# Expert blocks that gather and scatter token rows, and a final norm by token tiles

## The reference

```python
def hierarchical_moe(h, w_rg, b_rg, w_re, b_re, w_gate, w_up, w_down):
    p_g = softmax(hf @ w_rg + b_rg)                  # 4 groups
    g_sel = argmax(p_g); p_gsel = p_g[g_sel]
    e_logits = (hf @ w_re + b_re)[group g_sel]       # 8 experts of the group
    top_p, top_i = top_k(softmax(e_logits), 2)
    weights = top_p / sum(top_p) * p_gsel
    ...                                              # rows sorted by expert
    hid = silu(xb @ w_gate[e]) * (xb @ w_up[e])      # 1024 -> 512
    y = hid @ w_down[e]                              # 512 -> 1024
    out[token] += y * weight

x = x + g_f * hierarchical_moe(h, ...)               # g_f: 1024 gates
return rms_norm_2(x, final_norm_g)                   # x * rsqrt(mean(x*x) + eps) * g
```

## Time and profile before

| | us |
|---|---|
| median of 3 runs | 2663.51 (2662.41 to 2669.47) |
| the profiled execution, its own time | 2671.42 |
| its span in the profile | 2669.7 |
| TensorE busy | 2448.4 (92%) |
| VectorE busy | 814.4 (31%) |
| ScalarE busy | 472.3 (18%) |
| GpSimd busy | 35.3 (1%) |
| mean granted clock of TensorE | 0.955 of full speed |

### The profile page before, as it was taken

The page is one execution under the profiler, slowest core; times in us unless marked ns, Lnnn a source line. Parts: engine busy times, 40 slices in busy tenths (PEclk is TensorE's granted clock), DMA queues, the critical chain, the costliest instruction groups (busy, mean ns, idle before and its releaser), DMA issues. The chain is left out here.

```text
span 2669.7 us, 22222 instructions
## 1 busy us (share of the span) xinstructions
PE 2448.4 (92%) x8196; PEld 1209.4 (45%) x8196; DVE 814.4 (31%) x1821; ACT 472.3 (18%) x1005; POOL 35.3 (1%) x50
## 2 busy tenths in 40 slices
PE   6999899999999999989999999999994798888883
PEld 4444544444444655554444444645554333333331
DVE  4444331212123265552121221377423000000004
ACT  2322111110002154431111000112311010000000
POOL 0000000000000000000000000000001000000001
PEclk9999799999999899989999999999996899999996
DMA  8434113433342111214843343321006679999992
GB/s 329 173 142 163 74 63 126 163 151 127 131 184 103 56 56 55 81 64 159 328 176 138 126 164 151 126 91 36 1 0 262 257 323 428 428 429 428 428 401 111
DMA packets 50482, 482.53 MB, mean 181 GB/s; under 512 B 4928, under 2 KB 4928, under 8 KB 25296
## 3 DMA queue, kind: packets, MB, share of 16 engines
q1 hardware_dynamic: 36784, 430.85, 40.6%
q0 software_dynamic: 10112, 38.80, 3.8%
q10 hardware_dynamic: 3488, 11.58, 1.1%
HBM read 444.47 MB, written 36.74 MB: 180 GB/s over the span
## 5 line engine op out<-in xcount | busy, mean ns | idle before, releaser
L1021 PE MATMUL ps<-big,ring 128*128 128x512 f32 x1024 | 448.9, 596 | 3.6 <-PEq L932 1.5
L963 PE MATMUL ps<-hT,ring 128*128 128x512 f32 x1024 | 444.2, 594 | 0.0
L1021 PEld LDWEIGHTS ps<-big,ring 128*128 128x128 f32 x1024 | 192.6, 191 | 245.6 <-issue 245.6
L963 PEld LDWEIGHTS ps<-hT,ring 128*128 128x128 f32 x1024 | 193.9, 191 | 237.8 <-issue 236.6
L2529 PE MATMUL ps<-ring,big 128*64 128x512 f32 (+1 forms) x768 | 259.4, 603 | 25.1 <-ACT big L2575 10.8
L576 PE MATMUL ps<-hT,ring 128*128 128x512 f32 x384 | 174.8, 606 | 2.1 <-ACT hT L428 2.1
L2529 PEld LDWEIGHTS ps<-ring,big 128*64 128x64 f32 (+1 forms) x768 | 92.2, 154 | 156.6 <-issue 136.5
L2529 PE MATMUL ps<-big 128*64 128x512 f32 (+1 forms) x384 | 143.2, 625 | 19.1 <-DMA oT<-in_up 7.5
L1715 PE MATMUL ps<-hT,ring 128*128 128x512 f32 x320 | 142.4, 600 | 2.7 <-DVE big L2097 1.7
L206 DVE SCALAR_TENSOR_TENSOR tmp<-ring,cact,tmp 128x512 f32<-128x512 f32 (+1 forms) x192 | 131.6, 685 | 6.8
L2611 DVE TENSOR_TENSOR big<-big,ps 128x512 f32<-128x512 f32 x20 | 13.7, 687 | 349.4 <-ACT big L2579 333.0
(11 more groups left out here) (414 smaller groups left out, 2474.0 us busy)
## 6 DMA issues: line engine op xcount, KB each, us to landing
ring<-in_stream SPq DMA_DIRECT2D x99, 2048.0 KB, 8.8
ring<-in_gate SPq DMA_DIRECT2D x18, 2048.0 KB, 27.5
ring<-in_up SPq DMA_DIRECT2D x17, 2048.0 KB, 28.0
ring<-in_down SPq DMA_DIRECT2D x13, 2048.0 KB, 29.9
big<-in_down SPq DMA_DIRECT2D x10, 2048.0 KB, 29.4
big<-in_up SPq DMA_DIRECT2D x8, 2048.0 KB, 28.4
slot_rows<-zero POOLq DMA_DIRECT2D x2, 7424.0 KB, 38.6
big<-in_gate SPq DMA_DIRECT2D x6, 2048.0 KB, 30.4
```

Source lines behind the costliest of these rows:

```text
L963: last = pe.matmul(m.ps[:, j, :], w[:, k, j * P:(j + 1) * P], m.hT[:, k, :], start=(k == 0), stop=(k == KT - 1))
L1021: last = pe.matmul(m.ps[:, bank(half, j), :], w[:, k, j * P:(j + 1) * P], hid[:, 8 * c + k, :], start=(c == 0 and k == 0), stop=(c == 3 an ...
```

## The change

- Row tables. `m.d_xt` holds the 512 token rows in order, stored by ScalarE (`m.written`); there is no table of slots. The routing builds a table of places on TensorE: for each of 29 blocks and each of its 128 rows the token, the row of `m.d_yt` (token, or token + 512 for the second choice) and the weight. A place with no row gets 4096, which is beyond the bound, and its row isn't moved.
- Each block gathers its rows from `m.d_xt` by an indirect DMA on GpSimd, scales its output by weight and gate on VectorE and scatters it to `m.d_yt` by an indirect DMA on GpSimd. Only `m.d_yt` is filled with zeros, 4 MB.
- Block 0's rows are picked on TensorE by a matmul with a 0/1 matrix, and its gate and up products run inside the routing phase. The last block isn't scattered: TensorE spreads it by a 0/1 matrix to the four token tiles.
- Four weight loads go out in the residual phase (`HELD_EARLY`). The logits run with the feature tile in the outer loop. The group's Exp stands before the row evictions on ScalarE. Ranks come from comparisons with the expert on partitions, no longer from cubes.
- During blocks 1 to 8 TensorE turns the residual tile by tile to token rows. The rows of `m.d_yt` are loaded by SP and added before the last block's.
- The final norm goes by token tiles: ScalarE squares and sums a tile, VectorE scales it, SP stores it (0.5 MB). The output is now stored as tokens x features. The order of the last two blocks is `down(18)`, `front(19)`, `down(19)`, and the loads follow it.
- The overflow phase is rewritten with nine unrolled blocks and one set of buffers; it still doesn't run on this data.

```diff
@@ phase_residual
             def _(sp):
                 prefetch(m, sp, name)
+                if name == "out_m":
+                    for i in range(HELD_EARLY):
+                        load_expert(m, sp, i)
@@ phase_route, TensorE
-                keep_busy(m, pe, 5, 7)
-                for i in range(NT):
-                    for k in range(KT):
-                        pe.wait_ge(h_ok, k + 1)
+                for k in range(KT):
+                    gated = pe.matmul(..., m.mod2[:, 40 + k:41 + k].to_broadcast([P, P]), ident, ...)
+                for k in range(KT):
+                    pe.wait_ge(h_ok, k + 1)
+                    for i in range(NT):
...
+                pe.matmul(m.ps[:, 0, 0:NT * EXPERTS], con(m, "tri_strict"), whole, start=True, stop=True)
+                pe.matmul(m.ps[:, 1, 0:NT * EXPERTS], m.ones[:], whole, start=True, stop=True).then_inc(counted, 1)
...
+                pe.wait_ge(picked, NT)
+                for k in range(KT):
+                    for i in range(NT):
+                        last = pe.matmul(m.ps[:, 4 + k // 4, ...], rows[:, i, k * P:(k + 1) * P], pick[:, i, :], ...)
+                for j in range(2):
+                    pe.wait_ge(m.wfull[j], 16)
+                    for k in range(KT):
+                        if j == 0 and k == 2:
+                            for n in range(2 * NT):
+                                pe.wait_ge(tables, 1 + n // NT)
+                                last = pe.matmul(m.ps[:, 7, 0:3 * PL], row_of[:, n, :], table[:, n, :, :], ...)
+                            last.then_inc(tabled, 1)
+                        pe.matmul(m.ps[:, 2 + j, :], xt0[:, k * P:(k + 1) * P], bufs[j][:, k * 512:(k + 1) * 512], ...)
@@ phase_route, ScalarE
+                act.wait_ge(eg, 1)
+                act.activation(ge, ge, ACT.Exp).then_inc(expd, 1)
                 for i in range(NT):
                     act.activation(rows[:, i, :], ..., ACT.Copy).then_inc(ev, 1)
+                    act.dma_start(m.d_xt[i * P:(i + 1) * P, :], rows[:, i, :]).then_inc(m.written, 16)
-                act.wait_ge(eg, 1)
-                act.activation(ge, ge, ACT.Exp).then_inc(expd, 1)
@@ phase_route, GpSimd
-                        pool.indirect_dma_start(m.d_xs, bass.IndirectOffsetOnAxis(ap=m.idx[:, c:c + 1], axis=0),
-                                                rows[:, i, :], None).then_inc(m.scattered, 16)
+                pool.wait_ge(m.written, 16 * NT)
+                pool.wait_ge(xpick, 2)
+                pool.wait_ge(slotted, 1)
+                for t in (1, 2):
+                    gather_rows(m, pool, gathered_rows(m)[:, t % 2, :], PLACES[t]).then_inc(m.xin[t % 2], 16)
@@ phase_experts, GpSimd
-                    pool.dma_start(xb[:, t % 2, :], block_rows(m.d_xs, t)).then_inc(xin[t % 2], 16)
+                    if 3 <= t + 2 < BLOCKS:
+                        pool.wait_ge(xtr, t + 1)
+                        gather_rows(m, pool, xb[:, t % 2, :], PLACES[t + 2]).then_inc(m.xin[t % 2], 16)
+                    if t < last:
+                        pool.wait_ge(ya, t + 1)
+                        pool.wait_ge(yb, t + 1)
+                        pool.indirect_dma_start(m.d_yt, ..., y[:, t % 2, :], None, bounds_check=2 * T - 1,
+                                                oob_is_err=False).then_inc(yo[t % 2], 16)
@@ phase_experts, SP, behind the weight loads
+                sp.wait_ge(dn, last)
+                for i in range(NT):
+                    for j in range(2):
+                        sp.dma_start(yrows[j][:, i, :], m.d_yt[j * T + i * P:...]).then_inc(yin[i], 16)
+                tail.store(sp, 0)
@@ phase_experts, TensorE
+                    if 1 <= t <= KT:
+                        for i in range(NT):
+                            ins = pe.transpose(m.ps[:, 1, ...], m.xT[:, t - 1, i * P:(i + 1) * P], ident)
...
-                front(0)
                 for t in range(BLOCKS):
-                    if t + 1 < BLOCKS:
+                    if 1 <= t + 1 < last:
                         front(t + 1)
+                    elif t == last:
+                        front(t)
                     down(t)
+                for h, done in enumerate((ya, yb)):
+                    pe.wait_ge(done, BLOCKS)
+                    for i in range(NT):
+                        pe.matmul(m.ps[:, 2 * i + h, :], spread[:, i * P:(i + 1) * P], y[:, ..., h * 512:(h + 1) * 512], ...)
@@ phase_experts, VectorE
+                    for h, done in enumerate((ya, yb)):
+                        dve.scalar_tensor_tensor(y[:, s, ...], m.ps[:, 6 + h, :], m.wt[:, PLACES[t]:...],
+                                                 gate_rows(m)[:, ...], ALU.mult, ALU.mult).then_inc(done, 1)
...
+                for i in range(NT):
+                    dve.wait_ge(yin[i], 32)
+                    for j in range(2):
+                        c1.link(dve.tensor_tensor(token_rows(m, i), token_rows(m, i), yrows[j][:, i, :], ALU.add))
+                rows_out(last)
+                for h in range(2):
+                    for i in range(NT):
+                        dve.wait_ge(loose, NT * h + i + 1)
+                        add_rows(m, dve, i, h).then_inc(joined, 1)
+                        if h and i:
+                            tail.scaled(dve, i - 1, 0)
+                tail.scaled(dve, NT - 1, 0)
+class FinalNorm:
+    def squares(self, act, joined, before):
+        for i in range(NT):
+            act.activation(..., token_rows(m, i), ACT.Square, accum_out=m.st[:, i:i + 1]).then_inc(self.squared, 1)
+            act.activation(m.st[:, i:i + 1], m.st[:, i:i + 1], ACT.Sqrt, bias=m.eps[:, 0:1], scale=1.0 / D)
+    def scaled(self, dve, i, again):
+        dve.reciprocal(m.st[:, i:i + 1], m.st[:, i:i + 1]).then_inc(self.inverse, 1)
+        dve.scalar_tensor_tensor(self.out[:, i, :], token_rows(m, i), m.st[:, i:i + 1], final_gain(m), ALU.mult, ALU.mult)
@@ build
             lambda: phase_overflow(nc, m),
-            lambda: phase_combine(nc, m),
-            lambda: phase_norm(nc, m, "h", [(fl(m, "final_norm2"), None, None, m.hT)]),
-            lambda: phase_store(nc, m, out),
+            lambda: phase_stored(nc, m),
```

More of the change, by code:

```diff
@@ L2235, in _ @@
                 dve.reciprocal(m.st[:, 0:16], m.st[:, 0:16])
+HELD_EARLY = 4
 def load_order():
@@ L2300, in phase_route @@
     sc = take(NT * 8).rearrange("p (j i) -> p j i", j=8)
-    cnt, over, start, tmp32, incl, key, rank, base, cap, jump = (take(EXPERTS) for _ in range(10))
+    cnt, over, start, tmp32, incl, key, rank, base, cap, jump, less, more, at_rank = (take(EXPERTS) for _ in range(13))
+    key_rows, rank_rows = take(1), take(1)
+    ahead = take(NT * EXPERTS).rearrange("p (i n) -> p i n", i=NT)
+    first = take(NT)
     nbc = take(2)
@@ new lines, in _ @@
+                dve.tensor_reduce(block_of, step[:, :, 1:PL + 1], AX.X, ALU.add).then_inc(chn, 1)
+                c1.n += 1
+                c1.link(dve.tensor_tensor(in_block, step[:, :, 0:PL], step[:, :, 1:PL + 1], ALU.subtract))
+                c1.link(dve.scalar_tensor_tensor(block_of, block_of, -float(P), slot, ALU.mult, ALU.add))
+                for n, a in enumerate((con(m, "token"), con(m, "choice"), m.wts[:].rearrange("p j i -> p (j i)"))):
+                    dve.tensor_tensor(table[:, :, n, :], in_block, over_pl(a), ALU.mult).then_inc(chn, 1)
+                    c1.n += 1
@@ L2456, in _ @@
             def _(sp):
-                for i in range(WBUF):
+                for i in range(HELD_EARLY, WBUF):
                     if LOADS[i][2] >= PINNED:
@@ L2722, in step @@
-                    last.then_inc(dn, 1)
-                front(0, 0, 0)
-                walk(pe, step)
+                            ins = pe.matmul(m.ps[:, 6 + h, :], ht[:, k * P:(k + 1) * P],
+                                            bufs[2][:, k * D + h * 512:k * D + (h + 1) * 512], start=(k == 0), stop=(k == 3))
+                    ins.then_inc(dn, 1)
+                    pe.wait_ge(spread_ok, n + 1)
+                    for h, done in enumerate((ya, yb)):
+                        pe.wait_ge(done, n + 1)
+                        for i in range(NT):
+                            pe.matmul(m.ps[:, 2 * i + h, :], spread[:, i * P:(i + 1) * P], y[:, h * 512:(h + 1) * 512],
+                                      start=True, stop=True).then_inc(loose, 1)
```

623 lines of the change are left out of this document (315 added, 308 removed).

## The result

The kernel now takes **2585.9 us** (median of 4 runs, 2583.4 to 2587.4) against 2664.6 for the kernel before on the same chip: ratio 0.9701, 95% interval 0.9684 to 0.9718, faster by 78.6 us. The forecast was 2560 us in a range of 2542 to 2588, so some 104 us were expected and three quarters of them came. The profiled execution took 2587.35 us; its span is 2585.6, 84.1 less than before. Nothing ahead of the change differs between the two profiled executions: TensorE ends the products of the last residual phase at 2003.1 in both.

A forecast was written before the change was run, and what follows sets the result against it. Bounds by stage: what delays block 1 in routing, bytes in the experts, the chain of small steps at the end. Terms -40.9 - 26 + 2 - 38.6 = -103.5 gave span 2566, median 2560 us, range 2542 to 2588.

The forecast's parts named there:

- (a): Rival on gathers and scatters: places with no row still cost, so the 20 us stay, 2580 us; chance 0.12.
- (b): Rival on routing: TensorE stays at the low clock, block 1 comes 12 us later, 2572 us; chance 0.09.
- (d): Rival on the experts: TensorE, not DMA, binds from the start, 10 us more, 2570 us; chance 0.14.
- Routing, -40.9: Stage before block 1: shorter routing and earlier gathers start block 1 at 2060.6 instead of 2101.45, -40.9 us.
- the walk: Within routing: step times added up until the order of the experts is known, at 2032.5 against 2057.4.
- Expert bytes, -20: Expert blocks: only existing rows move, 6.6 MB instead of 15, so the DMA-bound stretch takes 423 us, -20 us.
- The last weights land: End of the expert blocks: last weights land 11 us before the last product instead of 17, -6 us.
- The new order of the last blocks, -6 on the last product: Last two blocks: the new order shortens last weights to last product from 17 to 11 us, -6 us.
- VectorE's adds, +2: Before the last rows are scaled: eight adds of expert rows on VectorE must be done first, +2 us (0 to 5).
- The end, 20 us: From last product to end of span, without the adds: 20 us instead of 58.6, -38.6 us.
- Rival (c): Expert blocks: gathers become the bound as VectorE keeps GpSimd from writing descriptors; 2722 us at 30 us landing; chance 0.03.

The follow-up runs named there:

- e6_norows: The changed kernel with the bound of both transfers by table set to row 0, so no gather or scatter moves more than one row: 27.5 us less by the medians.
- e5_order: The changed kernel with the last two blocks in the order of the kernel before: +6.5 us by the medians.
- e10_even: e8_deal with, besides, the rows of four single-expert blocks exchanged between lower and upper 64 partitions: 2579.5 us.
- e8_deal: The changed kernel with the places of a block dealt over the partitions by groups of four, only a row of constants changed: 2579.6 us.
- after: The changed kernel itself without further edit, against the kernel before: 2585.9 us, ratio 0.9701.
- e1_spread: The changed kernel with a first dealing, places spread over different groups of eight partitions within each half of 64: +3.3 us.

## Why the forecast was right and wrong

The time lies 26 us above the forecast and 2 us inside the range. That end of the range stood for the rivals (a), (b) and (d); neither (a) nor (b) came, and of (d) only a part. What took the time the range did not have in it, so that it held is in part luck.

By spans, 103.5 us were expected and 84.1 came. The routing gave 3.0 more than forecast, the blocks up to the last product 17.4 less (501.1 us for 509.7 before, where 484 were expected), the end 4.9 less (26.9 for 58.6, where 22 were expected). Another 5.5 of the difference lie in the medians: the execution profiled before stood 6.9 us above the median before, the one after 1.5, and the forecast took the saving in span off the median as it stood.

- **Routing, -40.9: right.** Measured -43.9 (2101.45 to 2057.6). The logits were done at 2018.9, between the high clock's 2017.5 and the 2020.5 that was taken, and the order came within 1.2 us of the walk. Rival (b), the low clock, did not come.
- **Expert bytes, -20: right.** The rows in the full stretch were 6.6 MB, as forecast, and DMA was full for 423 us. Before it was full for 446 and not 443, up to 2597. e6_norows shows that a row left out costs next to nothing. Rival (a) falls.
- **"The last weights land" is the step that failed.** Behind block 1's start the last load landed 499.7 us before (2601.1) and 490.2 after: 9.5 us sooner, not 26. Two things were wrong in it. First, the forecast let a load land when the DMA's mean work is done. The first engine was indeed done 20.9 us sooner (496.2, now 475.3), but the distance from it to the last engine grew from 3.5 to 14.9 us, and a load counts only with its last engine. Second, the 17 us from the last landing to the last product were misread: 2594 is the end of the stretch that was looked at, and the last load landed at 2601.1, 10.0 us ahead of the last product. So the 6 us that the new order was to save there did not exist: it is 10.9 us in the changed kernel and 11.1 with the old order (e5_order).

  Before the change, by stretch (same columns as above):

```profile
2151.00:2597.00 446.00, 391.73 (x1529) 154.88 (x1530) 34.23 (x50) 38.20 (x67) 7.91 (x15) 0.97 1.01 427
2597.00:2601.00 4.00, 4.00 (x10) 1.74 (x10) 0.00 (x0) 0.00 (x0) 0.00 (x0) 1.00 0.39 168
```

- **How much of this the uneven engines cost** is shown by the dealings: 501.9 us to the last product on the mean of four kernels, 498.2 and 496.4 with two dealings. That is some 5.5 of the 17 us. With e10_even the sum is 55.4 us until the DMA is full, 421.2 to the first engine, 7.9 to the last and 13.1 to the last product, 497.6; the forecast had 49.5, 423, nothing and 11. The other 12 us lie in the misread landing (7) and for the most part in the later start of the full stretch (3 to 6; it is 52.4 in the changed kernel).
- **Rival (d), TensorE binds, had a part of the truth.** The two nearly tie: TensorE waits for weights only once in three blocks, and each wait also costs it slower records behind it. But each of these waits ends with a load, so the DMA's slowest engine is what sets the pace, and not TensorE, until 2490.8; from there on it is TensorE.
- **The new order of the last blocks, -6 on the last product: wrong place.** In the old order the last product comes no later (500.1 us against 501.1 to 502.9). The order gives 6.5 us by the earlier scatter of block 18.
- **VectorE's adds, +2: measured +3.6**, within its bounds of 0 to 5, on the chain and removable.
- **The end, 20 us: 23.4 behind the adds.** Of the 3.4, 2.4 are the spread products at a granted clock of 0.73 (2562 to 2573), which the forecast took at the high clock's 0.43 a record.
- **Rival (c), gathers as the bound: no.** 16.7 us at most. Its rule, from the Trainium skill (DMA: Bandwidth & Descriptors, "SWDGE vs HWDGE vs iDMA"), that VectorE's two-port modes lock out the writing of descriptors, would show as long issues; scatters took 997 ns and gathers 1014 against 952 before, so the trace shows some 60 ns of it at most. The trace does not say which of VectorE's operations used such a mode, so no run here tests the rule itself.

Not settled: why the distance in e10_even is 7.4 us where evenly filled transfers leave 3.5 to 3.8, and how much of its 2 us over e8_deal is real. No run took work off TensorE to show what its 67.8 us behind the last wait are worth.

## What to carry to other kernels

A transfer by table that skips absent places saves their bytes, but it saves them on some of the sixteen engines only, and everything queued behind it ends with the engine that saved least. Look at when the first and the last engine finish one load before trusting a bound by mean bytes, and deal the used places over the partitions; here a row of constants gave about 4 us of the 17 that were missing. An order of blocks is to be judged by every output that leaves with a block, not by the last product alone.

## What the hardware showed unasked

- Which engine moved a partition's row in these 128-row transfers by table: the group of four partitions modulo 8, plus 8 for the upper 64. It fits the sixteen end times of the first gather under three placements (0 or 4; 0, 1, 3, 5, 7; 0 or 4 rows an engine) and the order of the drift in four kernels: by it the rows of the most and the least loaded engine are 30.6, 36.3, 18.3 and 2.9 us apart (after, e1_spread, e8_deal, e10_even; an estimate at 26.6 GB/s an engine), and measured were 17.6, 18.5, 15.0 and 7.4. The sizes don't fit, only the order.
- A skipped place still makes a packet, of 4 bytes and about 9 ns (2920 of them in the changed kernel, one for each absent place), where a 4,096-byte row takes about 160 ns.
- Engines can be 15 to 18 us apart while the mean share reads 1.01: a full DMA by the page says nothing about their being even.
